# Ordering an expert layer's weights gate, up, then the down of the pair before, with outputs combined in five groups

## The chip, the cores and the metric

The kernel runs on one core of a Trainium2 chip. The metric is the time of one execution on the device, in microseconds (us).

## What is computed

The reference is a stack of four layers over 512 tokens of width 1024, in float32. Two of them end in a mixture of 16 experts, and only these two stages matter here. Every expert takes the 64 tokens with the highest affinity for it; what it returns is weighted with the gate and added back to the tokens:

```
x_e  = the 64 tokens that expert e chose                 (64 x 1024)
y_e  = (silu(x_e @ w_exp_gate[e]) * (x_e @ w_exp_up[e])) @ w_exp_down[e]
x    = x + gt_f * sum over e of  gate_e * y_e, put back to the tokens of e
```

Each of the three matrices of an expert is 1024 x 1024 in float32, 4 MB, so that one expert layer reads 192 MB of weights and uses each number for 64 tokens.

## The kernel before, in words

The engines run programs of their own, joined by semaphores. `Due` (line 182) counts for each engine how often it has already waited for a name, so that `due("y_sb")` is "the next y_sb".

**Weights.** All weights of the program are a list of panels, written in the order of their use; `expert_panels` (line 448) writes the part of an expert layer: 192 panels of 1,024 KB. The ring in SBUF has 8 slots. SP (line 513) issues one transfer per panel, in the order of the list, and before panel n it waits until TensorE has freed panel n - 8. TensorE takes panels in the same order with `panel()` (line 546). A product frees its panels through `free[0]`: the number is given to the next matmul that carries no signal of its own (line 531). Transposes (`turn`, line 541) never do this, and a matmul with a signal does not either.

**The expert stage.** The 16 experts go in 8 pairs p. A pair's two sets of 64 tokens stand side by side as 128 columns. On TensorE (`experts`, line 1063) the loop over pairs (line 1144) goes:

- `pair(0, x_sel, ...)`: the gate product into banks 0 and 1 of PSUM. A product takes 8 panels in four sub-steps of two panels.
- pairs 0 and 1: `turn_gates` (line 1096), which turns two tiles each of the gate weights through banks 6 and 7.
- pairs 3, 4, 6 and 7: `combine_blocks` (line 1134) for the outputs of three earlier pairs and half of the 8 feature blocks, through banks 6 and 7 in turn. VectorE adds each finished block to x (`add`, line 2156), and TensorE goes back to a bank after that.
- `pair(2, x_sel, ...)`: the up product into banks 2 and 3.
- `gather(p + 1)` (line 1105): the tokens of the next pair, 32 matmuls of 128 columns, into banks 6 and 7.
- the wait for `e_act`, the 8 transposes of the activations into banks 0 and 1, the wait for their copy (`aT_sb`), and `pair(4, e_actT, ...)`: the down product into banks 4 and 5.

After the loop the last two pairs are combined for all 8 blocks (line 1165).

ScalarE (line 1636) takes for each pair three steps on the gate (Exp, Ln, Exp; lines 1638 to 1640), the copies of the turned gates (1643), of the gathered tokens (1633), of the turned activations (1648), and of the down product into `y_store` (1650), which has room for 8 pairs. VectorE (line 2396) multiplies the gate in (2402), adds combined blocks to x (2405) and multiplies with up (2407).

Of the kernel before, what the change touches and what calls it, by code (L numbers as in the profile page):

```python
# [12 lines left out]
ACT = mybir.ActivationFunctionType  # L13
# [5 lines left out]
P = 128  # L19
D = 1024  # L20
KB = D // P
T = 512
# [261 lines left out]
def build(nc, args, out, par):  # L284
    a = args
    general, first_t, even_t, pool_t = (packed(t)[1] for t in constants())
    with ExitStack() as ctx:
# [30 lines left out]
        def cut(buffer, start, size, **shape):  # L318

            v = buffer[:, start:start + size]  # L320
            if not shape:
                return v
            names_ = " ".join(shape)
            return v.rearrange(f"p ({names_}) -> p {names_}", **shape)
# [77 lines left out]
        r_affT, r_thr_rows = two(work, 6144), work[:, 7168:7296]  # L402
        h_tok, sel = cut(mixflat, 0, 4096, n=4, f=D), cut(work, 0, 4096, n=4, c=D)
        r_pg, x_sel, e_act = work[:, 6144:7168], cut(work, 4096, 1024, k=KB, c=P), work[:, 5120:6144]
        r_pgT, y_store = cut(hbuf, 0, 4096, i=8, t=T), cut(proj_all, 0, 8192, i=8, d=D)
        e_actT, e_tmp = cut(proj_all, 8192, 1024, k=KB, c=P), proj_all[:, 9216:10240]


# [38 lines left out]

        def expert_panels(l):

            for e in range(0, E, 2):  # L450
                for w in ("w_exp_gate", "w_exp_up", "w_exp_down"):
                    for j in range(4):
                        for s in range(2):
                            v = a[w][l, e + s, 2 * j * P:(2 * j + 2) * P, :]
                            panels.append((v.rearrange("(k p) n -> p k n", p=P), 2, D))

        by_columns(a["w_in_even"][0], 2832)
        modulation_panels(PLANS["even"])
# [29 lines left out]
        def rounded(v):  # L488
# [1 line left out]
            return bass.AP(tensor=halves_of[v.tensor.name], offset=v.offset, ap=v.ap)  # L490


        combining = {3: (range(0, 3), range(0, 4)), 4: (range(0, 3), range(4, 8)),
                     6: (range(3, 6), range(0, 4)), 7: (range(3, 6), range(4, 8))}
        gate_tiles = {0: (0, 1), 1: (2, 3)}
        last_pairs = range(6, 8)

        def make_link(eng, name):

# [22 lines left out]
        def _(pe):  # L522
# [3 lines left out]
            def mm(o, lhsT, rhs, start, stop, signal=None, **kw):  # L526

                i = pe.matmul(o, lhsT, rhs, start=start, stop=stop, **kw)  # L528
                if signal:
                    i.then_inc(sem[signal], 1)  # L530
                elif free[0]:
                    i.then_inc(sem["panel_used"], free[0])
                    free[0] = 0
# [7 lines left out]
            def turn(o, i, signal=None, n=P):  # L541
                t = pe.transpose(o, i, ident[0:n, 0:n])  # L542
                if signal:
                    t.then_inc(sem[signal], 1)
# [518 lines left out]
            def experts(l):  # L1063
# [32 lines left out]
                def turn_gates(tiles):  # L1096

                    for n in tiles:
                        pe.wait_ge(*due("r_pg"))
                        for p in range(8):  # L1100
                            turn(ps[:, 6 + p // 4, p % 4 * P:p % 4 * P + P], r_pg[:, p * P:p * P + P],
                                 "r_pgT" if p == 7 else None)
                        pe.wait_ge(*due("r_pgT_sb"))
# [9 lines left out]
                def pair(banks, lhs, signal):  # L1113

                    for j in range(4):
                        w = [panel(), panel()]
                        for kk in range(2):
                            k = 2 * j + kk
                            for half in range(2):
                                for e in range(2):  # L1120
                                    s = slice(e * 64, e * 64 + 64)
                                    mm(ps[s, banks + half, :], lhs[:, k, s], w[e][:, kk, half * 512:half * 512 + 512],
                                       k == 0, k == KB - 1, signal if k == KB - 1 and half and e else None)
                        free[0] += 2

                unread = [0]

                def combine(pairs, m, bank):

                    for p in pairs:  # L1130
                        mm(ps[:, bank, :], y_store[:, p, m * P:m * P + P], r_pgT[:, p, :], p == pairs[0], p == pairs[-1],
                           "down" if p == pairs[-1] else None)

                def combine_blocks(pairs, blocks):
                    for m in blocks:
                        if unread[0] == 2:
                            pe.wait_ge(*due("down_x"))
                            unread[0] -= 1
                        combine(pairs, m, 6 + m % 2)
                        unread[0] += 1  # L1140

                pe.wait_ge(*due("r_marks"))
                gather(0)
                for p in range(8):
                    pe.wait_ge(*due("x_sel_sb"))
                    pair(0, x_sel, "e_gate")
                    turn_gates(gate_tiles.get(p, ()))
                    if p:
                        pe.wait_ge(*due("y_sb"))
                    if p in combining:  # L1150
                        combine_blocks(*combining[p])
                    pair(2, x_sel, "e_up")
                    if p < 7:
                        if unread[0]:
                            pe.wait_ge(*due("down_x", unread[0]))
                            unread[0] = 0
                        gather(p + 1)
                    pe.wait_ge(*due("e_act"))
                    for k in range(KB):
                        turn(ps[:, k // 4, k % 4 * P:k % 4 * P + P], e_act[:, k * P:k * P + P], "aT" if k == KB - 1 else None)  # L1160
                    pe.wait_ge(*due("aT_sb"))
                    pair(4, e_actT, "e_down")
                pe.wait_ge(*due("y_sb"))
                pe.wait_ge(*due("down_x", unread[0]))
                for m in range(KB):
                    combine(last_pairs, m, m)
                due("down_x", KB)

            def pooling():
# [81 lines left out]
        def _(act):  # L1251
# [367 lines left out]
            def experts():  # L1619
                act.wait_ge(*due("r_sub"))  # L1620
                to("r_exp", f(r_aff, r_aff, ACT.Exp))
                for i in range(8):
                    n, half = i // 2, i % 2
                    act.wait_ge(*due("r_tok"))
                    to("r_tok_sb", f(h_tok[:, n, half * 512:half * 512 + 512], ps[:, 4 + half, :], ACT.Copy))
                act.wait_ge(*due("r_affT"))
                to("r_affT_sb", f(r_affT[0:E, 0, :], ps[0:E, 1, :], ACT.Copy))
                act.wait_ge(*due("r_thr_rows"))
                to("r_thr_sb", f(r_thr, ps[:, 2, 0:E], ACT.Copy))

                def selected():
                    act.wait_ge(*due("x_sel"))
                    to("x_sel_sb", f(x_sel, ps[:, 6:8, :].rearrange("p b (i c) -> p (b i) c", i=4), ACT.Copy))  # L1633

                selected()
                for p in range(8):
                    act.wait_ge(*due("e_gate"))
                    link(f(e_tmp, ps[:, 0:2, :].rearrange("p b f -> p (b f)"), ACT.Exp, scale=-1.0))
                    link(f(e_tmp, e_tmp, ACT.Ln, bias=1.0))
                    to("e_exp", f(e_tmp, e_tmp, ACT.Exp, scale=-1.0))  # L1640
                    for n in gate_tiles.get(p, ()):
                        act.wait_ge(*due("r_pgT"))
                        to("r_pgT_sb", f(r_pgT[:, :, n * P:n * P + P],
                                         ps[:, 6:8, :].rearrange("p b (i t) -> p (b i) t", i=4), ACT.Copy))
                    if p < 7:
                        selected()
                    act.wait_ge(*due("aT"))
                    to("aT_sb", f(e_actT, ps[:, 0:2, :].rearrange("p b (i c) -> p (b i) c", i=4), ACT.Copy))  # L1648
                    act.wait_ge(*due("e_down"))
                    to("y_sb", f(y_store[:, p, :], ps[:, 4:6, :].rearrange("p b f -> p (b f)"), ACT.Copy))  # L1650

            def layer(l):
                if l:
# [82 lines left out]
        def _(dve):  # L1736
# [607 lines left out]
            def experts(gate):  # L2344
# [51 lines left out]
                for p in range(8):  # L2396
                    for n in gate_tiles.get(p, ()):
                        dve.wait_ge(*due("r_pgT"))
                        if n < NT - 1:
                            gated(n + 1)  # L2400
                    dve.wait_ge(*due("e_exp"))
                    link(tt(e_tmp, e_tmp, ps[:, 0:2, :].rearrange("p b f -> p (b f)"), ALU.mult))  # L2402
                    if p in combining:
                        for m in combining[p][1]:
                            add(gate, m, 6 + m % 2, "down", "down_x")
                    dve.wait_ge(*due("e_up"))
                    to("e_act", tt(e_act, e_tmp, ps[:, 2:4, :].rearrange("p b f -> p (b f)"), ALU.mult))

            def pooling():

# [134 lines left out]
```

## Time and profile before

| what | value |
|---|---|
| time before, median of 3 runs | 3923.52 us (3921.61 to 3927.85) |
| the profiled execution's own time | 3919.22 us |
| its span, first to last instruction | 3917.4 us |
| TensorE matmuls busy | 3312.8 us (85%) |
| VectorE busy | 1424.9 us (36%) |
| ScalarE busy | 932.7 us (24%) |
| read from HBM | 632.48 MB, 162 GB/s over the span |
| mean granted clock of TensorE | 0.906 |

The shares are over the whole program, in which stages with different limits follow each other. The two expert stages are the last but one group of slices and the last group; they alone stream weights at nearly 400 GB/s, while the stages between them read little. "PE" is TensorE's matmuls, "PEld" its weight loads, "DVE" VectorE, "ACT" ScalarE, "SPq" the queue of SP. A float32 matmul stands in the trace as two records. Line 528 is the helper that issues every matmul, line 542 the one of every transpose, so products are told apart by what they read: `ring,work` is a gate or up product, `ring,proj` a down product, `work,mix` the gathering, `h,proj` the combining.

### The profile page before, as it was taken

How to read it: one execution, taken by the hardware profiler on the slowest of the kernel's cores; microseconds unless marked ns; L12 is line 12 of the kernel's file. 1: busy time of each engine (PE TensorE's matmuls, PEld its weight loads, DVE VectorE, ACT ScalarE, POOL GpSimd, SP SyncE). 2: the span in 40 equal slices, each digit the busy share in tenths (PEclk: the TensorE clock that was granted, in tenths of full speed). 3: DMA queues.
4: the chain of work that ended last, by engine and by line, in shares of the span. 5: the costliest groups of instructions: out<-in, count | busy, mean ns of one | idle time of the engine just before them, and what ended most of it. 6: DMA issues, size and time to landing. Idle time of an engine off the chain costs nothing. (4 is left out here: it accounts for less than half of the span.)

```text
span 3917.4 us, 38069 instructions
## 1 busy us (share of the span) xinstructions
PE 3312.8 (85%) x16560; PEld 2204.8 (56%) x16560; DVE 1424.9 (36%) x1841; ACT 932.7 (24%) x1395; POOL 0.2 (0%) x4
## 2 busy tenths in 40 slices
PE   6986879998996779999898967578898986789897
PEld 3765758886765766887454726454434344434342
DVE  3446437653546636762002365730000024200001
ACT  3542132233633223221203511111010021010101
POOL 0000000000000000000000000000000000000000
PEclk9996989999996989999998967679999997899999
DMA  6370012322261012323111090018999950499996
GB/s 228 96 269 1 1 42 88 97 86 79 86 238 63 1 33 76 97 92 109 44 54 33 3 401 27 4 39 321 395 389 391 382 213 32 192 396 390 395 384 238
DMA packets 247383, 637.05 MB, mean 163 GB/s; under 512 B 12849, under 2 KB 110129, under 8 KB 247089
## 3 DMA queue, kind: packets, MB, share of 16 engines
q1 hardware_dynamic: 244128, 627.22, 43.0%
q10 hardware_dynamic: 3088, 7.40, 0.5%
q8 instruction: 131, 2.15, 0.2%
q14 instruction: 36, 0.29, 0.0%
HBM read 632.48 MB, written 2.10 MB: 162 GB/s over the span
## 5 line engine op out<-in xcount | busy, mean ns | idle before, releaser
L528 PE MATMUL ps<-ring,work 128*64 128x512 f32 (+1 forms) x3584 | 585.7, 542 | 137.8 <-DMA ring<-in_w_exp_gate 51.2
L528 PE MATMUL ps<-mix_halves,work_halves 128*128 128x512 f32 (+1 forms) x1456 | 585.4, 402 | 29.6 <-DVE h_halves L1790 29.5
L528 PE MATMUL ps<-h_halves,work_halves 128*128 128x512 f32 (+1 forms) x1456 | 573.3, 394 | 34.5 <-DVE mix_halves L1790 34.5
L528 PE MATMUL ps<-mix_halves,ring_halves 128*128 128x512 f32 x1264 | 495.1, 392 | 0.0
L528 PEld LDWEIGHTS ps<-ring,work 128*64 128x64 f32 (+1 forms) x3584 | 207.0, 133 | 501.1 <-issue 401.7
L1790 DVE TENSOR_TENSOR ring_halves<-ring,work_halves 128x2048 fp32r<-128x2048 f32 x108 | 239.1, 2214 | 302.4 <-ACT work_halves L1273 301.6
L528 PEld LDWEIGHTS ps<-mix_halves,work_halves 128*128 128x128 f32 (+1 forms) x1456 | 274.9, 189 | 110.3 <-issue 30.8
L528 PEld LDWEIGHTS ps<-h_halves,work_halves 128*128 128x128 f32 (+1 forms) x1456 | 275.9, 189 | 99.6 <-issue 42.6
L1273 ACT ACTIVATE work_halves<-ring 128x2048 fp32r<-128x2048 f32 x108 | 199.6, 1849 | 487.3 <-PE ps L528 390.9
L528 PEld LDWEIGHTS ps<-mix_halves,ring_halves 128*128 128x128 f32 x1264 | 237.9, 188 | 52.3
L528 PE MATMUL ps<-ring,proj 128*64 128x512 f32 x1024 | 226.4, 600 | 18.5 <-ACT proj L1648 16.2
L2402 DVE TENSOR_TENSOR proj<-proj,ps 128x1024 f32<-128x1024 f32 x16 | 19.5, 1220 | 530.2 <-ACT proj L1640 522.5
L1752 DVE RECIPROCAL work<-work 128x512 f32<-128x512 f32 (+1 forms) x56 | 181.4, 3239 | 1.9
L528 PE MATMUL ps<-work,proj 128*128 128x128 f32 (+1 forms) x912 | 148.8, 321 | 38.2 <-DVE work L2122 13.8
L528 PE MATMUL ps<-h,proj 128*128 128x512 f32 (+2 forms) x384 | 166.7, 576 | 4.6 <-issue 2.3
L528 PE MATMUL ps<-h,ring 128*128 128x512 f32 (+1 forms) x368 | 161.8, 598 | 5.6 <-ACTq L1264 5.6
L528 PEld LDWEIGHTS ps<-ring,proj 128*64 128x64 f32 x1024 | 73.8, 138 | 160.8 <-issue 141.3
L528 PEld LDWEIGHTS ps<-work,proj 128*128 128x128 f32 (+1 forms) x912 | 129.2, 213 | 57.2 <-issue 15.6
L528 PE MATMUL ps<-work,consts 128*128 128x512 f32 (+1 forms) x188 | 110.5, 738 | 49.8 <-ACT work L1307 34.4
L542 PE MATMUL ps<-consts,work 128*128 128x128 f32 x530 | 87.8, 310 | 70.4 <-DVE work L2364 24.4
L528 PE MATMUL ps<-proj_halves,work_halves 128*128 128x512 f32 x352 | 136.9, 389 | 0.0
L528 PEld LDWEIGHTS ps<-work,mix 128*128 128x128 f32 x1024 | 119.8, 198 | 22.1 <-issue 11.4
(354 smaller groups left out, 3602.9 us busy)
## 6 DMA issues: line engine op xcount, KB each, us to landing
ring<-in_w_exp_gate SPq DMA_DIRECT2D x128, 1024.0 KB, 8.8
ring<-in_w_exp_up SPq DMA_DIRECT2D x128, 1024.0 KB, 13.0
ring<-in_w_exp_down SPq DMA_DIRECT2D x128, 1024.0 KB, 10.5
ring<-in_ada_w SPq DMA_DIRECT2D x48, 1024.0 KB, 9.2
ring<-in_w_mod SPq DMA_DIRECT2D x48, 1024.0 KB, 16.8
ring<-in_w_in SPq DMA_DIRECT2D x22, 1024.0 KB, 5.3
ring<-in_w_gate SPq DMA_DIRECT2D x22, 1024.0 KB, 5.3
ring<-in_w_up SPq DMA_DIRECT2D x22, 1024.0 KB, 5.4
```

The lines of the kernel that those rows point to most:

```text
L528: i = pe.matmul(o, lhsT, rhs, start=start, stop=stop, **kw)
L542: t = pe.transpose(o, i, ident[0:n, 0:n])
L1273: to("hi", f(rounded(panel_high(splits[0])), slot(n), ACT.Copy))
L1752: link(dve.reciprocal(v, v))
L1790: to("lo", tt(rounded(v), v, rounded(hi), ALU.subtract))
L2402: link(tt(e_tmp, e_tmp, ps[:, 0:2, :].rearrange("p b f -> p (b f)"), ALU.mult))
```

## The change

Pairs are pipelined by one product: the down product of pair p - 1 comes after the up product of pair p, and the panels are listed in that order. The activations of pair p - 1 are turned between gate p and up p, into banks 6 and 7. Turning the gate tiles moves behind the up product. `y_store` keeps four pairs. Combining comes in five groups: pairs 0 and 1 before up 3, pairs 2 and 3 before up 5, pairs 4 and 5 before up 7, each over all 8 blocks; pair 6 before down 7, in four banks; pair 7 at the end. Each group but the last now ends with a wait until VectorE has added its last blocks.

```diff
-        r_pgT, y_store = cut(hbuf, 0, 4096, i=8, t=T), cut(proj_all, 0, 8192, i=8, d=D)
+        r_pgT, y_store = cut(hbuf, 0, 4096, i=8, t=T), cut(proj_all, 0, 4096, i=4, d=D)
...
         def expert_panels(l):
-            for e in range(0, E, 2):
-                for w in ("w_exp_gate", "w_exp_up", "w_exp_down"):
-                    for j in range(4):
-                        for s in range(2):
-                            v = a[w][l, e + s, 2 * j * P:(2 * j + 2) * P, :]
-                            panels.append((v.rearrange("(k p) n -> p k n", p=P), 2, D))
+            def product(w, p):
+                for j in range(4):
+                    for s in range(2):
+                        v = a[w][l, 2 * p + s, 2 * j * P:(2 * j + 2) * P, :]
+                        panels.append((v.rearrange("(k p) n -> p k n", p=P), 2, D))
+
+            for p in range(8):
+                product("w_exp_gate", p)
+                product("w_exp_up", p)
+                if p:
+                    product("w_exp_down", p - 1)
+            product("w_exp_down", 7)
...
-        combining = {3: (range(0, 3), range(0, 4)), 4: (range(0, 3), range(4, 8)),
-                     6: (range(3, 6), range(0, 4)), 7: (range(3, 6), range(4, 8))}
+        combining = {3: (0, 1), 5: (2, 3), 7: (4, 5)}
         gate_tiles = {0: (0, 1), 1: (2, 3)}
-        last_pairs = range(6, 8)
...
-                unread = [0]
-
                 def combine(pairs, m, bank):
                     for p in pairs:
-                        mm(ps[:, bank, :], y_store[:, p, m * P:m * P + P], r_pgT[:, p, :], p == pairs[0], p == pairs[-1],
+                        mm(ps[:, bank, :], y_store[:, p % 4, m * P:m * P + P], r_pgT[:, p, :], p == pairs[0], p == pairs[-1],
                            "down" if p == pairs[-1] else None)
-                def combine_blocks(pairs, blocks):
-                    for m in blocks:
-                        if unread[0] == 2:
+                def combine_blocks(pairs, banks):
+                    for m in range(KB):
+                        if m >= banks[1]:
                             pe.wait_ge(*due("down_x"))
-                            unread[0] -= 1
-                        combine(pairs, m, 6 + m % 2)
-                        unread[0] += 1
+                        combine(pairs, m, banks[0] + m % banks[1])
+                    pe.wait_ge(*due("down_x", banks[1]))
+
+                def turn_act():
+                    for k in range(KB):
+                        turn(ps[:, 6 + k // 4, k % 4 * P:k % 4 * P + P], e_act[:, k * P:k * P + P], "aT" if k == KB - 1 else None)
...
                 for p in range(8):
                     pe.wait_ge(*due("x_sel_sb"))
+                    if p:
+                        pe.wait_ge(*due("e_act"))
                     pair(0, x_sel, "e_gate")
-                    turn_gates(gate_tiles.get(p, ()))
-                    if p:
+                    if p >= 2:
                         pe.wait_ge(*due("y_sb"))
                     if p in combining:
-                        combine_blocks(*combining[p])
+                        combine_blocks(combining[p], (6, 2))
+                    if p:
+                        turn_act()
                     pair(2, x_sel, "e_up")
+                    if p:
+                        pe.wait_ge(*due("aT_sb"))
+                    turn_gates(gate_tiles.get(p, ()))
                     if p < 7:
-                        if unread[0]:
-                            pe.wait_ge(*due("down_x", unread[0]))
-                            unread[0] = 0
                         gather(p + 1)
-                    pe.wait_ge(*due("e_act"))
-                    for k in range(KB):
-                        turn(ps[:, k // 4, k % 4 * P:k % 4 * P + P], e_act[:, k * P:k * P + P], "aT" if k == KB - 1 else None)
-                    pe.wait_ge(*due("aT_sb"))
-                    pair(4, e_actT, "e_down")
+                    if p:
+                        pair(4, e_actT, "e_down")
+                pe.wait_ge(*due("e_act"))
+                turn_act()
                 pe.wait_ge(*due("y_sb"))
-                pe.wait_ge(*due("down_x", unread[0]))
+                combine_blocks((6,), (0, 4))
+                pe.wait_ge(*due("aT_sb"))
+                pair(4, e_actT, "e_down")
+                pe.wait_ge(*due("y_sb"))
                 for m in range(KB):
-                    combine(last_pairs, m, m)
+                    combine((7,), m, m)
                 due("down_x", KB)
```

On ScalarE the copy of the turned activations now stands right behind the three steps on the gate, and the copy of the down product of pair p - 1 behind that of the gathered tokens (for p = 7, and once more at the end). On VectorE the adds of a group cover all 8 blocks and stand, as before, behind the multiplication at line 2402; 8 adds of pair 6 follow the loop.

## Rows read from the trace of the kernel before

**Rows 1.** The page: the span, and the issues of the gate panels.

```profile
span 3917.4 us, 38069 instructions
...
ring<-in_w_exp_gate SPq DMA_DIRECT2D x128, 1024.0 KB, 8.8
```

**Rows 2.** Windows of the first expert stage; last columns: granted clock, DMA share, GB/s.

```profile
2660.60:3121.50 460.90, 406.46 (x1989) 178.03 (x1985) 29.68 (x29) 46.58 (x46) 0.00 (x0) 0.98 0.98 388
2660.60:2859.20 198.60, 170.24 (x860) 75.69 (x856) 10.91 (x9) 22.18 (x22) 0.00 (x0) 0.96 0.99 392
2886.00:2896.00 10.00, 8.85 (x70) 6.89 (x70) 0.00 (x0) 1.94 (x2) 0.00 (x0) 1.00 1.03 410
...
2873.50:2877.00 3.50, 3.50 (x20) 1.22 (x18) 0.00 (x0) 0.00 (x0) 0.00 (x0) 1.00 0.54 142
2939.50:2942.00 2.50, 2.50 (x14) 0.85 (x12) 0.00 (x0) 0.00 (x0) 0.00 (x0) 1.00 0.87 247
3067.50:3072.00 4.50, 4.50 (x24) 1.51 (x22) 0.00 (x0) 0.00 (x0) 0.00 (x0) 1.00 0.27 66
...
2897.00:2900.50 3.50, 3.50 (x18) 1.15 (x16) 0.00 (x0) 0.00 (x0) 0.00 (x0) 1.00 0.39 104
...
3092.00:3096.00 4.00, 4.00 (x22) 1.40 (x20) 0.00 (x0) 0.00 (x0) 0.00 (x0) 1.00 0.41 100
```

**Rows 3.** TensorE in order of time, gate 3 to down 3: start us, us.

```profile
2855.66 3.65 PE L528 MATMUL ps<-ring,work 128*64 128x512 f32 x16 [1.47 <-DMA ring<-in_w_exp_gate]
2859.25 10.82 PE L528 MATMUL ps<-h,proj 128*128 128x512 f32 x24
2870.00 13.95 PE L528 MATMUL ps<-ring,work 128*64 128x512 f32 x64
2883.88 7.41 PE L528 MATMUL ps<-work,mix 128*128 128x128 f32 x64
2891.13 1.04 PE L542 MATMUL ps<-consts,work 128*128 128x128 f32 x8
2893.32 13.95 PE L528 MATMUL ps<-ring,proj 128*64 128x512 f32 x64 [1.16 <-ACT proj L1648]
```

**Rows 4.** TensorE's waits, first expert stage: total us, times, longest us.

```profile
PE ps L528 <- DMA ring<-in_w_exp_gate: 26.1, 18, 2.8
```

**Rows 5.** TensorE in order of time, from the end of gate 7.

```profile
3121.48 10.82 PE L528 MATMUL ps<-h,proj 128*128 128x512 f32 x24
...
3147.51 1.09 PE L542 MATMUL ps<-consts,work 128*128 128x128 f32 x8 [1.32 <-DVE work L2407]
...
3166.40 13.97 PE L528 MATMUL ps<-h,proj 128*128 128x512 f32 x32 [1.16 <-issue]
```

**Rows 6.** ScalarE and VectorE in order of time, after gate 3.

```profile
2859.36 1.03 ACT L1638 ACTIVATE proj<-ps 128x1024 f32<-128x1024 f32 x1 [17.52 <-PE ps L528]
...
2861.50 1.06 ACT L1640 ACTIVATE proj<-proj 128x1024 f32<-128x1024 f32 x1
...
2862.59 1.22 DVE L2402 TENSOR_TENSOR proj<-proj,ps 128x1024 f32<-128x1024 f32 x1 [43.81 <-ACT proj L1640]
2863.84 1.61 DVE L2158 SCALAR_TENSOR_TENSOR x<-ps,small,x 128x512 f32<-128x512 f32 x2
```

**Rows 7.** TensorE around the gate tiles of pair 0; SP's first refill; landing times.

```profile
2668.10 1.09 PE L542 MATMUL ps<-consts,work 128*128 128x128 f32 x8
...
2675.51 15.38 PE L528 MATMUL ps<-ring,work 128*64 128x512 f32 x64 [1.16 <-issue]
...
2658.75 0.88 SPq L516 DMA_DIRECT2D ring<-in_w_exp_up  x2
...
DMA to landing us min/median/max: 4.8/8.8/13.7
```

**Rows 8.** TensorE behind its longest wait for panels, and the window of those sub-steps.

```profile
2793.32 8.78 PE L528 MATMUL ps<-ring,work 128*64 128x512 f32 x32 [2.77 <-DMA ring<-in_w_exp_gate]
...
2794.50:2797.90 3.40, 3.40 (x10) 1.21 (x8) 0.00 (x0) 0.00 (x0) 0.00 (x0) 0.50 1.03 411
```

More of the change, by code:

```diff
@@ L1633, in selected, with turned, stored @@
                     to("x_sel_sb", f(x_sel, ps[:, 6:8, :].rearrange("p b (i c) -> p (b i) c", i=4), ACT.Copy))
+                def turned():
+                    act.wait_ge(*due("aT"))
+                    to("aT_sb", f(e_actT, ps[:, 6:8, :].rearrange("p b (i c) -> p (b i) c", i=4), ACT.Copy))
+                def stored(p):
+                    act.wait_ge(*due("e_down"))
+                    to("y_sb", f(y_store[:, p % 4, :], ps[:, 4:6, :].rearrange("p b f -> p (b f)"), ACT.Copy))
                 selected()
@@ L1640, in experts @@
                     to("e_exp", f(e_tmp, e_tmp, ACT.Exp, scale=-1.0))
+                    if p:
+                        turned()
                     for n in gate_tiles.get(p, ()):
@@ L1646, in experts @@
                         selected()
[L1647 to L1650, printed above, removed]
+                    if p:
+                        stored(p - 1)
+                turned()
+                stored(7)
             def layer(l):
@@ L2403, in experts @@
                     if p in combining:
-                        for m in combining[p][1]:
+                        for m in range(KB):
                             add(gate, m, 6 + m % 2, "down", "down_x")
@@ L2407, in experts @@
                     to("e_act", tt(e_act, e_tmp, ps[:, 2:4, :].rearrange("p b f -> p (b f)"), ALU.mult))
+                for m in range(KB):
+                    add(gate, m, m % 4, "down", "down_x")
             def pooling():
```

## The prediction

> **What bounds the kernel now.** I read the page's head first [rows 1]: the profiled execution spans 3917.4 us, and its own time was 3919.2 us, 4.3 us under the median of the three runs (3923.5 us). The sum below is a difference, made on the profiled execution and then put on the median. Only the two expert stages change; the first runs from 2654 to 3180 us, the second has the same instructions, and the sum is made once and doubled.
>
> Next come the windows of the queue [rows 2]. While it is fed, the queue moves 410 GB/s, so a panel of 1,024 KB (1.049 MB) takes 2.56 us. From the first refill (2660.6 us) to the last panel of gate 7 that TensorE has to wait for (about 3121.5 us) the mean is 388 GB/s: the queue stands still for 460.9 x (1 - 388/410) = 24.7 us of 460.9. A pair of experts takes 24 panels, 24 x 2.56 = 61.4 us of queue, and costs TensorE less than that: the weights bound this stage. TensorE's list shows the same from its side: before a gate product's sub-steps it waits for panels some 1.47 us each [rows 3], 26.1 us in 18 waits before gate panels [rows 4].
>
> So the stage's length is: panels x 2.56, plus the queue's standstills, plus what TensorE does after the last panel it waited for. The ring holds 8 panels, 20.5 us of queue. A standstill comes where TensorE frees nothing for so long that all 8 slots fill. I call any stretch between two products a pause.
>
> **What a pause costs.** After gate 3 the pause is the combining, 2859.25 to 2870.00 = 10.75 us [rows 3]. The queue's dips after three such pauses are 3.5 x (1 - 142/410) = 2.3, 2.5 x (1 - 247/410) = 1.0 and 4.5 x (1 - 66/410) = 3.8 us [rows 2], mean 2.4; the fourth is like the first. By then the ring is full, so each further microsecond of pause is a microsecond of standstill: after a product that was itself waiting for panels, **idle = pause - 8.4**. A second kind of dip follows the pause for gather and turn, 2883.88 to 2893.32 = 9.4 us, entered with panels in hand: 2.6, 2.6 and 3.0 us (first and last of three in [rows 2]), so idle = pause - 6.7. The rest is at the start: 198.6 x (1 - 392/410) = 8.7 us until gate 3 ends.
>
> **The change, part by part (one expert stage).**
>
> *The long pause between gate and up in pairs 3, 5 and 7.* It now holds 8 blocks of two matmuls, in two banks, and the turning of the activations. A matmul of 512 columns costs 13.97/16 = 0.87, back to back 0.86 us [rows 5] (the profile lists each as two records). Blocks 0 and 1 take 3.4 us. Block 2 needs VectorE's add of block 0, and this stands behind the chain Exp, Ln, Exp on ScalarE and a multiply on VectorE: the chain starts at 2859.36, the add at 2863.84 and the pair of adds takes 1.61 us [rows 6], so TensorE can go on at 5.6 us after the gate's end: 2.2 us of waiting (with three matmuls a block this wait was only some 0.5 us). Blocks 2 to 7: 6 x 1.72 = 10.3. The new wait for both last adds: 0.9 (0.75 of add and its signals). Behind it on TensorE is the turning, 1.04 [rows 3], and behind this the up product; nobody else waits. Sum 3.4 + 2.2 + 10.3 + 0.9 + 1.04 = 17.9 us against 10.75. Idle 17.9 - 8.4 = 9.5 us, three times: **28.5 us**.
>
> *The pause between up and down, pairs 1 to 6.* The turning and the wait for its copy (1.15 us, end of turn to 2893.32) leave it; gather alone is 2883.88 to 2891.13 = 7.3 us. Behind an up product that was short of panels that is under 8.4: no dip. Behind the full ring after pairs 3 and 5 it is 7.3 - 6.7 = 0.6 us, twice: **1.2 us**. Moved activations, their copy and the x_sel copy lie under whole products of 13.95 us; were that cover gone, each would cost about 1.2 us.
>
> *The start.* Turning two gate tiles moves from behind gate 0 (and 1) to behind up 0 (and 1). It took 2668.10 to 2675.51 = 7.4 us [rows 7], of which some 2.5 us was waiting for ScalarE's chain; this is long done behind the up product. Two turns of 1.04, a copy or gate multiply between (1.3) and the copy after (1.15) give 4.6; I take 5.0, with 7.4 as the other end. Pauses then: 5.0 + 7.3 + 1.15 (the x_sel copy, uncovered here) = 13.4 before gate 1, and 12.3 before down 0. Idle 5.0 + 3.9 = **8.9 us**, against 8.7 now: the same.
>
> *The queue in all:* 28.5 + 1.2 + 8.9 = 38.6 us against 24.7: **+13.9 us**. SP issues the same 192 transfers, in another order; its wait for a slot stays the only one in that queue.
>
> *The tail.* Now the last panel that TensorE waits for belongs to gate 7; from this product's end to the last combining it is 3121.48 to 3166.40 + 13.97 = 58.9 us [rows 5]. After the change the last such panel is down 6's, 8 panels later (**+20.5 us**), and then come: the y_sb copy with the turning beside it 1.16, 8 matmuls 6.9, the last add 0.9, down 7 13.95, the copy 1.16, 8 matmuls 6.9 = 30.9 us, **-28.0 us**. In that pause nothing frees the last two slots, since its matmuls all carry a signal of their own and transposes free nothing: down 7's last two panels are issued only at its first matmul. From issue to landing a transfer takes 4.8 us at least [rows 7], plus 2.56 for the second and about 1 until the issue: 8.4 us, needed after 10.5 us. Covered, by 2 us.
>
> *Sum.* +13.9 + 20.5 - 28.0 = **+6.4 us a stage, +13 us in all**: 3919.2 + 13 = 3932 for the profiled execution, 3923.5 + 13 = **3936.5 us** on the median, 0.33% slower. A measurement of this kernel can tell about 0.2% (7.8 us) from no change.
>
> **Unknowns and their ends.** The 2.2 us wait inside the combining may cost the clock too: behind a wait of 2.77 us the sub-steps took 8.78 us for 32 records, not 7.0, at a granted clock of 0.50, the lower level, 1.2 GHz [rows 8]. That is 1.7 us in each long pause, at most +10 in all; other waits of 1.5 us are followed by full clock, so I take nothing. The gate tiles at 7.4 instead of 5.0: +4.8 a stage, +10 in all. The other way, the smallest dip seen (1.0) instead of 2.4: -4.2 a stage, -8 in all.
>
> **The rivals.**
> 1. *Forecast: the ring runs full in three long pauses.* For it: each shorter pause of the same place already shows a dip. 0.55, with 3925 to 3946 as its own range.
> 2. *The same, and the half clock in the pauses or the long gate tiles.* +13 + 10 to 20 = +23 to +33: 3946 to 3956. For it: the row at 0.50 clock; against: the many waits near 1.5 us keep the full clock. 0.13.
> 3. *The dips don't grow one for one* (the smallest dips, cheap gate tiles): +6.4 - 4.2 = +2 a stage, 3928, no change. 0.18.
> 4. *Other side: TensorE's own path is what counts.* Per stage it loses 7 waits for the copy (8.1), the wait for the last activations (1.3 [rows 5]) and 4.8 at the gate tiles; it gains 1.15 at x_sel and, in combining, 3 x 16.9 + 8.9 - 1.2 + 6.9 = 65.3 against 4 x 10.8 + 14.0 = 57.2, +8.1. Net -5.0, -10 in all: 3913.5. It decides if panel waits (26.1 us for gate panels) do not grow with the longer pauses, which needs a queue with spare time: 24.7 us of standstill says that there is a little, 61.4 us a pair that there is not much. 0.14.
>
> On the rate, the trace shows 410 GB/s [rows 2]. The Trainium skill (DMA: Bandwidth & Descriptors, Where 436 GB/s comes from) puts the ceiling at 435 GB/s. By that rule a panel would be 2.40 us, an estimate: the ring would be full 1.3 us sooner, at seven dry places after against twelve now (-6.5 us), and the 8 panels of the tail 1.3 us cheaper, so the sum would be about -1 us a stage, no change. No window here holds that rate; it would be one more way to rival 3.
>
> That the change does not do what it says is not to be feared: the order of panels and products is in the code.
>
> **How the numbers follow.** Slower by over 0.2% is rivals 1 and 2 less the edge of 1: 0.65. Within 0.2%: rival 3 and that edge, 0.22. Faster: 0.13. The range, 3911 to 3956, takes in the ends above and rival 4's value.
>
> **What the changed profile would show.** In each stage: three pauses of about 18 us from a gate's end to the first matmul of the up product, with block 2 waiting about 2 us for VectorE; a dip of 8 to 10 us in the queue behind each; the dips behind gather nearly gone; mean rate from first refill to down 6's last panel about 377 GB/s (176 x 1.049 MB in 176 x 2.56 + 38.6 us); 31 us from down 6 to the end of combining. The prediction is wrong if these dips are short, if up 0 does not wait for panels, or if down 7 waits for its last pair.

## The result, and the profile after

The changed kernel takes 3935.7 us (median of 9 runs, 3929.9 to 3943.8) against 3923.5 us before (9 runs, 3915.5 to 3927.9): ratio 1.0033, 95% interval 1.0022 to 1.0044. It is slower, by a third of a percent. The profiled execution took 3929.9 us, with a span of 3928.1 us.

The two expert stages, from the first matmul of gate 0 to the last combining, took 526.2 and 523.3 us before and take 530.9 and 529.4 us now, 10.8 us more in all. The rest of the program is the same, 2867.9 and 2867.7 us. So the whole difference of the two spans, 10.7 us, lies in the two stages.

TensorE in order of time after the change, gate 3 to down 2, and then the end of the stage (start us, us, instruction, in brackets the idle time before it and what ended it); it answers to [rows 3] and [rows 5]:

```profile
2836.39 3.65 PE L532 MATMUL ps<-ring,work 128*64 128x512 f32 x16 [1.47 <-DMA ring<-in_w_exp_gate]
2839.97 3.70 PE L532 MATMUL ps<-h,proj 128*128 128x512 f32 x8
2845.37 10.57 PE L532 MATMUL ps<-h,proj 128*128 128x512 f32 x24 [1.70 <-DVE x L2178]
2856.78 1.10 PE L546 MATMUL ps<-consts,work 128*128 128x128 f32 x8 [0.84 <-DVE x L2178]
2857.81 13.95 PE L532 MATMUL ps<-ring,work 128*64 128x512 f32 x64
2871.69 7.41 PE L532 MATMUL ps<-work,mix 128*128 128x128 f32 x64
2879.04 13.95 PE L532 MATMUL ps<-ring,proj 128*64 128x512 f32 x64
...
3154.88 1.09 PE L546 MATMUL ps<-consts,work 128*128 128x128 f32 x8
3156.07 7.13 PE L532 MATMUL ps<-h,proj 128*128 128x512 f32 x16
3164.09 13.95 PE L532 MATMUL ps<-ring,proj 128*64 128x512 f32 x64 [0.89 <-issue]
3179.16 7.13 PE L532 MATMUL ps<-h,proj 128*128 128x512 f32 x16 [1.11 <-ACT proj L1651]
```

The second row is blocks 0 and 1 of the combining, the third blocks 2 to 7, after a wait for VectorE's add. From the gate's end to the up product it is 2857.81 - 2839.97 = 17.8 us, against 10.75 before. At the end, down 7 runs through its 64 records without a wait for panels.

The windows of the same stage after the change (columns as in [rows 2]): first refill to the end of down 6; first refill to the end of gate 3; the two dips of the start; then, in order of time, the three long dips and the two dips behind gather.

```profile
2661.60:3154.90 493.30, 429.23 (x2077) 186.98 (x2073) 40.89 (x43) 49.25 (x48) 0.00 (x0) 0.99 0.95 378
2661.60:2840.00 178.40, 153.11 (x789) 69.51 (x785) 10.91 (x9) 20.46 (x20) 0.00 (x0) 0.98 0.98 389
2700.00:2709.00 9.00, 9.00 (x44) 3.02 (x46) 0.00 (x0) 0.00 (x0) 0.00 (x0) 1.00 0.67 251
2745.00:2754.00 9.00, 9.00 (x50) 3.74 (x50) 0.00 (x0) 1.03 (x1) 0.00 (x0) 1.00 0.47 167
2853.00:2866.00 13.00, 12.15 (x53) 4.58 (x53) 1.80 (x3) 1.02 (x1) 0.00 (x0) 1.00 0.33 121
2883.00:2887.00 4.00, 4.00 (x22) 1.39 (x20) 0.00 (x0) 0.00 (x0) 0.00 (x0) 1.00 0.88 317
2986.00:2999.00 13.00, 12.15 (x55) 4.67 (x55) 1.70 (x3) 1.02 (x1) 0.00 (x0) 1.00 0.36 123
3015.00:3020.00 5.00, 5.00 (x26) 1.72 (x24) 0.00 (x0) 0.00 (x0) 0.00 (x0) 1.00 0.94 342
3119.00:3132.00 13.00, 12.15 (x55) 4.73 (x55) 1.61 (x3) 1.02 (x1) 0.00 (x0) 1.00 0.34 121
```

At 410 GB/s as the full rate, each long dip is 13 x (1 - 121/410) = 9.2 us of standstill, where the kernel before had 1.0 to 3.8 us. The dips behind gather are down to 4 x (1 - 317/410) = 0.9 and 5 x (1 - 342/410) = 0.8 us. In all the queue stands still for 493.3 x (1 - 378/410) = 38.5 us, against 24.7. The granted clock in the windows of the long dips is 1.00.

### The profile page after: what moved, and what is told of

Read it like the earlier page. It is cut to its first block and busy times, and to the rows that moved or that the text cites. A ratio compares the mean times of both kernels' runs of the same rounds, so it can differ in the third digit from the quotient of the medians.

```text
span 3928.1 us, 38102 instructions
## 1 busy us (share of the span) xinstructions
PE 3307.7 (84%) x16560; PEld 2205.9 (56%) x16560; DVE 1449.0 (37%) x1873; ACT 933.7 (24%) x1395; POOL 0.2 (0%) x4
## 5 line engine op out<-in xcount | busy, mean ns | idle before, releaser
L532 PE MATMUL ps<-work,proj 128*128 128x128 f32 (+1 forms) x912 | 149.2, 322 | 38.3 <-DVE work L2142 13.9
L532 PE MATMUL ps<-h,proj 128*128 128x512 f32 (+2 forms) x384 | 166.3, 576 | 14.9 <-DVE x L2178 10.2
L2178 DVE SCALAR_TENSOR_TENSOR x<-ps,small,x 128x512 f32<-128x512 f32 x128 | 93.4, 749 | 178.1 <-PE ps L532 174.5
L532 PE MATMUL ps<-work,consts 128*128 128x512 f32 (+1 forms) x188 | 108.6, 728 | 49.8 <-ACT work L1317 34.4
L532 PE MATMUL ps<-work,mix 128*128 128x128 f32 x1024 | 124.3, 285 | 15.4 <-DVE work L2406 10.6
## 6 DMA issues: line engine op xcount, KB each, us to landing
ring<-in_w_exp_up SPq DMA_DIRECT2D x128, 1024.0 KB, 12.3
```

Of the source, the lines that this page charges most:

```text
L2178: to(done, stt(out=x[:, m, :], in0=ps[:, bank, :], scalar=gate[:, m:m + 1], in1=x[:, m, :], op0=ALU.mult, op1=ALU.add))
```

## The experiments

All are compared by their medians, with the kernel before run on the same chip beside them (its medians there were 3920.9 to 3922.7 us); the ratios are against that. Where a few microseconds matter, the lengths of the two expert stages in the profiles are given as well, since what lies outside them moved between 2867 and 2879 us from one profile to the next, without any edit there. The changed kernel was not run beside them. The kernel before was 0.8 to 2.7 us faster there than the 3923.5 us above, so a difference between a run's median and the changed kernel's 3935.7 us is uncertain by about as much.

**1. Half groups.** The same outputs are combined in two halves of four blocks.

```diff
-        combining = {3: (0, 1), 5: (2, 3), 7: (4, 5)}
+        combining = {3: ((0, 1), range(0, 4)), 4: ((0, 1), range(4, 8)), 5: ((2, 3), range(0, 4)),
+                     6: ((2, 3), range(4, 8)), 7: ((4, 5), range(0, 4))}
...
+                    if p == 7:
+                        combine_some((4, 5), range(4, 8), late_banks)
```

> The changed kernel, but each group of two pairs is combined in two halves of four blocks (pairs 3 to 7, and once behind up 7), still in two banks. Ring theory (idle of the queue = pause - 8.4 us behind a gate product): the pause becomes 3.4 + 2.2 + 3.4 + 0.9 + 1.04 = 11.0 us, so 2.6 us of standstill five times and 0.6 us behind gather four times, 24.5 us a stage instead of 38.6: 28 us less in all than the changed kernel, about 3908 us. Rival, TensorE's own path sets the time: five waits for VectorE of 3.1 us instead of three, so 12 us more than the changed kernel, about 3948 us.

Measured: 3911.1 us, ratio 0.9970 (0.9958 to 0.9981). More waits for VectorE, and still 25 us less than the changed kernel. The rival, which wanted 3948, is out. Four of the five dips in that profile:

```profile
2922.00:2929.00 7.00, 7.00 (x34) 2.29 (x32) 0.00 (x0) 0.00 (x0) 0.00 (x0) 1.00 0.81 297
2986.00:2994.00 8.00, 8.00 (x40) 2.59 (x38) 0.00 (x0) 0.52 (x1) 0.00 (x0) 1.00 0.79 291
3052.00:3058.00 6.00, 6.00 (x30) 2.00 (x28) 0.00 (x0) 0.00 (x0) 0.00 (x0) 1.00 0.73 267
3116.00:3122.00 6.00, 6.00 (x30) 2.00 (x28) 0.00 (x0) 0.00 (x0) 0.00 (x0) 1.00 0.81 293
```

They are 1.9, 2.3, 2.1 and 1.7 us, where 2.6 were expected; the first, behind gate 3, is 16 x (1 - 347/410) = 2.5 us.

**2. Six banks.** The long groups stay whole, but the blocks go to banks 4, 5, 2, 3, 6, 7.

```diff
+        some_banks = (4, 5, 2, 3, 6, 7)
...
-                        combine_blocks(combining[p], (6, 2))
+                        combine_some(combining[p], range(KB), some_banks)
+                        read(4)
```

> The changed kernel with its three long groups whole, but over six banks (4, 5, 2, 3, 6, 7), so that no matmul waits for an add inside the pause. Ring theory: the pause falls from 17.8 to 6.9 + 6.9 + 1.04 = 14.8 us, the standstill from 9.1 to 6.2 us, 18 us less in all: about 3917 us. If the clock or the wait itself were the cost and not the length of the pause, the queue's dip would keep its 9 us.

Measured: 3916.4 us, ratio 0.9985 (0.9974 to 0.9996). TensorE's list and the windows of the three dips:

```profile
2844.17 14.00 PE L533 MATMUL ps<-h,proj 128*128 128x512 f32 x32
2858.01 1.04 PE L547 MATMUL ps<-consts,work 128*128 128x128 f32 x8
```

```profile
2857.00:2867.00 10.00, 10.00 (x49) 3.91 (x49) 1.00 (x2) 1.02 (x1) 0.00 (x0) 1.00 0.40 146
2987.00:2997.00 10.00, 10.00 (x49) 3.91 (x49) 0.84 (x2) 1.02 (x1) 0.00 (x0) 1.00 0.45 163
3117.00:3127.00 10.00, 10.00 (x50) 3.87 (x51) 0.75 (x1) 1.02 (x1) 0.00 (x0) 1.00 0.44 160
```

The wait is gone from the combining, the pause is 2858.98 - 2844.17 = 14.8 us, and the dips are 6.4, 6.0 and 6.1 us. It is the length of the pause that counts.

**3. Both.** Half groups over banks 2, 3, 4, 5 (and 0, 1, 6, 7 behind up 7). As in run 2, the waits for the adds that are still open stand behind the up product.

> As the kernel in halves, but the four blocks go into four banks that are free at that time, so TensorE waits for no add inside the pause. Ring theory: pause 6.9 + 1.04 = 7.9 us, below 8.4, no standstill behind gate products or gather; only the 9 us at the start stay. 29.5 us a stage less than the changed kernel, 59 in all: about 3877 us (3870 to 3890). Rival, TensorE's own path: only the waits go, 3 x 3.0 us a stage, 18 us in all: about 3918 us.

Measured: 3881.5 us, ratio 0.9901 (0.9886 to 0.9916), with all the work done. One pause and the window around it, and the window from the first of these pauses to down 6:

```profile
2837.21 7.13 PE L534 MATMUL ps<-h,proj 128*128 128x512 f32 x16
2844.18 1.04 PE L548 MATMUL ps<-consts,work 128*128 128x128 f32 x8
2845.15 13.95 PE L534 MATMUL ps<-ring,work 128*64 128x512 f32 x64
```

```profile
2840.00:2853.00 13.00, 13.00 (x57) 5.24 (x57) 4.04 (x5) 1.54 (x2) 0.00 (x0) 1.00 1.03 410
...
2837.00:3127.00 290.00, 273.06 (x1291) 116.31 (x1290) 29.30 (x34) 29.01 (x28) 0.00 (x0) 1.00 1.02 408
```

The pause is 7.9 us, and the queue runs through it at 410 GB/s. For 290 us it loses next to nothing (408 of 410).

**4. No combining of pairs 0 to 5.** `combining = {}`.

> The changed kernel without the combining of pairs 0 to 5 (their outputs are not added to x; pairs 6 and 7 are). Takes 16.8 us of TensorE out of three pauses of a stage, 50 us a stage. Ring theory: only the queue's standstill can be won, 3 x 9.1 + 2 x 0.6 = 28.5 us a stage, 57 in all: about 3879 us, and the waits for panels grow. Rival, TensorE's own path: 101 us less, about 3835 us.

Measured: 3878.2 us, ratio 0.9892 (0.9877 to 0.9906). 50 us of TensorE's work and waiting taken out of each stage, 101 in all, gave 57 us, about what the queue had stood still in the pauses (3 x 9.2 + 0.9 + 0.8 = 29.3 us a stage). The waits for the panels of up products grew from 22.1 us (in the changed kernel) to

```profile
PE ps L532 <- DMA ring<-in_w_exp_up: 34.9, 27, 2.9
```

Run 3 does all the combining and is only 3 us slower than this.

**5. Four more matmuls, in the long pauses or in the short ones.** `mm(ps[:, 6, :], y_store[:, 0, 0:P], r_pgT[:, 0, :], True, True)` four times, at the end of the combining, or between gate and up of pairs 2, 4 and 6.

> The changed kernel with four further matmuls (3.4 us, into a bank that is written anew) at the end of the combining in pairs 3, 5 and 7. Ring theory: those pauses already fill the ring, each grows from 17.8 to 21.3 us, and all of it is standstill: 3.4 x 6 = 21 us more than the changed kernel, about 3956 us. TensorE's own path says the same here; it is the pair to dup_short.

> The changed kernel with the same four matmuls between gate and up of pairs 2, 4 and 6, where the pause is only 1.04 us. Ring theory: 4.5 us is below 8.4, the ring does not fill, TensorE only waits less for panels: no change, about 3936 us. Rival, TensorE's own path: 21 us more, about 3956 us.

Measured: 3956.4 us (ratio 1.0090, 1.0074 to 1.0105) in the long pauses, 3937.1 us (1.0035, 1.0022 to 1.0048) in the short ones. The same 24 matmuls cost 21 us in one place and 1.4 us, within the spread of the runs, in another (23.6 and 3.5 us by the lengths of the stages). First the dips of the former, then three windows of the latter over the lengthened short pauses:

```profile
2856.00:2872.00 16.00, 15.15 (x64) 5.74 (x65) 0.75 (x1) 1.02 (x1) 0.00 (x0) 1.00 0.27 96
2992.00:3008.00 16.00, 15.15 (x64) 5.82 (x64) 1.12 (x2) 1.03 (x1) 0.00 (x0) 1.00 0.26 91
```

```profile
2780.00:2792.00 12.00, 12.00 (x52) 4.85 (x50) 1.22 (x1) 4.16 (x4) 0.00 (x0) 1.00 1.03 410
2914.00:2926.00 12.00, 12.00 (x53) 4.84 (x51) 1.22 (x1) 4.16 (x4) 0.00 (x0) 1.00 1.03 410
3046.00:3058.00 12.00, 12.00 (x52) 4.87 (x50) 1.22 (x1) 4.16 (x4) 0.00 (x0) 1.00 1.02 409
```

**6. The old order without that combining.** The kernel before with `combining = {}`.

> The kernel before, old order, without the combining of pairs 0 to 5 (not added to x; pairs 6 and 7 are at the end). It stands to the run no_mid (3878 us) as the order alone. Ring theory: the pause of gather, turning and copy is 9.4 us behind an up product that waits for panels, 1.0 us of standstill in six pairs, 8.7 at the start, so 10 us less than in the kernel before; and the tail falls by 4.4 us (up 7 now waits for panels): 14.4 us a stage, 29 in all, about 3893 us, 15 us above no_mid. Rival, the order is worth nothing: as no_mid, 3878 us. If TensorE's path set the time, 44 us of combining a stage would be won, about 3835 us.

Measured: 3899.4 us, ratio 0.9940 (0.9923 to 0.9956), 21 us above run 4. The two stages took 512.3 and 510.3 us, 26.9 us less than in the kernel before (28.8 expected); the rest of the difference from 3893 us is outside them (2875.5 us in this profile). So the new arrangement is worth some 20 us where nothing of pairs 0 to 5 is combined (by the stages: 512.3 + 510.3 against 501.9 + 502.2, 18.5 us), and the changed kernel gives it back. The expectation's "order alone" says too much: run 4 also turns the gate tiles behind the up product, and it combines pair 6 before down 7, where the old kernel combines pairs 6 and 7 at the end. The ends of the first stage, from the last of its first 184 panels on, first in this run and then in run 4:

```profile
3136.09 3.65 PE L527 MATMUL ps<-ring,work 128*64 128x512 f32 x16 [1.46 <-DMA ring<-in_w_exp_up]
...
3161.46 13.97 PE L527 MATMUL ps<-h,proj 128*128 128x512 f32 x32 [1.16 <-issue]
```

```profile
3124.50 3.65 PE L532 MATMUL ps<-ring,proj 128*64 128x512 f32 x16 [1.44 <-DMA ring<-in_w_exp_down]
...
3152.36 7.13 PE L532 MATMUL ps<-h,proj 128*128 128x512 f32 x16 [1.11 <-ACT proj L1651]
```

That tail is 35.7 us here and 31.3 us in run 4 (35.9 and 31.3 in the second stage): 8.9 us of the 18.5. The other 9.7 lie before it, 476.7 us from the stage's start against 470.6, and 474.4 against 470.8; the queue stands still there for 474.9 x (1 - 398/410) = 13.9 us in the first stage here and 464.5 x (1 - 403/410) = 7.9 us in run 4.

**7. Pair 6 combined at the end.**

```diff
-                combine_blocks((6,), (0, 4))
...
-                    combine((7,), m, m)
+                    combine((6, 7), m, m)
```

> The changed kernel with pair 6 combined together with pair 7 at the end, instead of before down 7. By the ledger of the queue: the pause before down 7 shrinks from 9.2 to 2.2 us, but down 7 then waits for its panels (its last pair lands 20.5 us after down 6's), so it ends 20.5 us after down 6, and 1.2 + 13.9 us of combining follow: 35.6 us from down 6 to the last combining instead of 31.4. 4.2 us more a stage, 8 in all, about 3944 us. Rival, TensorE's own path: the same matmuls in another place, one wait of 0.9 us less, about 3934 us.

Measured: 3950.4 us, ratio 1.0064 (1.0042 to 1.0086). The sign and the mechanism are those of the ledger (the sum over the queue and the tail), the size is not: 14.7 us more than the changed kernel by the medians, 13.3 by the stages, not 8. The end of the second stage in that profile:

```profile
3890.55 1.09 PE L546 MATMUL ps<-consts,work 128*128 128x128 f32 x8
3892.94 3.65 PE L532 MATMUL ps<-ring,proj 128*64 128x512 f32 x16 [1.30 <-DMA ring<-in_w_exp_down]
3897.20 3.65 PE L532 MATMUL ps<-ring,proj 128*64 128x512 f32 x16 [0.61 <-DMA ring<-in_w_exp_down]
3902.32 3.65 PE L532 MATMUL ps<-ring,proj 128*64 128x512 f32 x16 [1.47 <-DMA ring<-in_w_exp_down]
3908.17 5.35 PE L532 MATMUL ps<-ring,proj 128*64 128x512 f32 x16 [2.20 <-DMA ring<-in_w_exp_down]
3914.73 13.97 PE L532 MATMUL ps<-h,proj 128*128 128x512 f32 x32 [1.21 <-ACT proj L1650]
```

Down 7 now waits for its panels, as expected. In the second stage its last sub-step waits 2.2 us and then takes 5.35 instead of 3.65 us, at a granted clock of 0.72 in the window from 3908 to 3914 us, and this tail is 38.2 us, not 35.6. In the first stage no sub-step is slow, and it is 36.9 us: down 7 starts 6.3 us after the sub-step before it, where the panels of two sub-steps take 5.12 us of queue. Against 31.4 us in each stage of the changed kernel the tails give 12 of the 13 us, the two stages taken together (by stage they gave 5.5 and 6.8 us, and the stages grew by 3.5 and 9.7).

**8. The second gate tile through banks 4 and 5,** on top of run 3.

```diff
-                            turn(ps[:, 6 + p // 4, p % 4 * P:p % 4 * P + P], r_pg[:, p * P:p * P + P],
+                            turn(ps[:, 6 - 2 * (n % 2) + p // 4, p % 4 * P:p % 4 * P + P], r_pg[:, p * P:p * P + P],
...
-                        pe.wait_ge(*due("r_pgT_sb"))
+                        if n % 2 == 0:
+                            pe.wait_ge(*due("r_pgT_sb"))
```

> The kernel of halves_banks (3881 us), with the second gate tile of a pair turned into banks 4 and 5, so that its copy is waited for only before the down product. The pauses at the start fall from 13.3 and 12.1 us by about 1.2 us each. Ring theory: 1.2 us less standstill twice a stage, 5 us in all, about 3877 us; it is the only standstill left. If the start is not what bounds the rest, no change: 3881 us.

Measured: 3877.9 us, ratio 0.9887 (0.9873 to 0.9902). It is 3.6 us below run 3, but the ranges of the two (3879.2 to 3884.9 and 3874.3 to 3881.3) overlap. The two pauses of the first stage did shrink as expected, from 13.3 and 12.1 to 11.9 and 10.6 us. The stages are less clear: the first took 504.2 us against 503.6 in run 3, the second 500.9 against 506.7, and 3.0 of those 5.8 us are a gathering that took 10.29 us in run 3 and 7.31 here. So the shorter pauses are shown, and their gain in time is not. It is the fastest version found, 1.1% faster than the kernel before and 58 us faster than the changed one, with all the work done.

## Why the prediction was right

The forecast was 3936.5 us, and 3935.7 us was measured. The number alone would prove little, since a sum of gains and losses can agree by chance; the parts and the runs say whether it did.

- **The bound.** The queue of weights bounds the stage. Run 5 shows it (the same work free in one place, at full price in another), and run 4 (101 us of TensorE's path removed, 57 gained).
- **The long pause.** 17.9 us worked out, 17.8 measured: the first wait is 1.70 us (2.2 in the sum), the wait at the end 0.84 (0.9), and blocks 2 to 7 are 10.57 us in the profile (10.3).
- **Idle = pause - 8.4.** The rule said 9.5 us a dip, and 9.2 came. The kernels give it five points and a bound, all behind a gate product that waited for panels:

| kernel | pause, us | mean standstill, us | pause less standstill |
|---|---|---|---|
| half groups, four banks | 7.9 | 0 | at least 7.9 |
| before | 10.75 | 2.4 | 8.4 |
| half groups | 11.0 | 2.1 | 8.9 |
| six banks | 14.8 | 6.2 | 8.6 |
| changed | 17.8 | 9.2 | 8.6 |
| four more matmuls | 21.3 | 12.3 | 9.0 |

  From 11 to 21 us of pause the standstill grows by 10.2 us: one for one. The constant is nearer to 8.8 than to the 8.4 that three uneven dips gave.
- **The pause for gather.** 0.6 us twice was forecast, 0.9 and 0.8 were measured.
- **The start.** 8.9 us forecast, 178.4 x (1 - 389/410) = 9.1 measured, but this agreement is partly luck. The pause before gate 1 is 13.3 us (13.4), and its dip is 3.5 us (9 x (1 - 251/410)), where pause - 8.4 gave 5.0: the rule doesn't hold there, and why was not tested. The pause before down 0 is 13.7, not 12.3, and its dip 5.3 (9 x (1 - 167/410)), not 3.9: gather took 9.01 us there instead of 7.4, with a granted clock of 0.76 in the window from 2737 to 2744 us. The two misses cancel.
- **The queue in all.** 38.6 us forecast, 38.5 measured in the first stage, 491.7 x (1 - 380/410) = 36.0 in the second.
- **The tail.** 30.9 us forecast, 3179.16 + 7.13 - 3154.88 = 31.4 measured. Down 7's last two panels were in time, as worked out. Run 7 shows that the place of pair 6's combining matters as the ledger says.
- **The sum.** +6.4 us a stage; +4.8 and +6.1 measured, +10.8 in all instead of +13. Most of what is missing is in the first stage. From the first refill to the last panel waited for, it took 493.3 us against 460.9, 32.4 more, where 13.9 + 20.5 = 34.4 were forecast; the tail fell by 27.5, not 28.0. Whether the standstill or the 8 panels were the smaller can't be told: the rates are rounded to 1 GB/s, which is 1.2 us over 490 us.

Of the rivals, the half clock inside the pause did not come: after the 1.70 us wait, 24 records took 10.57 us, 0.44 us each, as without a wait. Nor did the long gate tiles: the two turns with their waits took 2691.40 - 2686.63 = 4.8 us, near the 5.0 of the sum. The length of one wait does not settle the clock. In run 7 the sub-step behind a wait of 2.2 us was slow (5.35 us); in the changed kernel's first stage the one behind a wait of 3.00 us, at 2728.88 us, took the usual 3.65 us. The dips that do not grow one for one are refuted by the table. TensorE's own path as the bound is refuted by runs 1, 4 and 5. The Trainium skill's ceiling of 435 GB/s (DMA: Bandwidth & Descriptors, Where 436 GB/s comes from) would, as a rate and by the estimate in the prediction, have meant no change. This stream does not reach it: over 290 us almost without a standstill (run 3) the queue moved 408 GB/s.

Of the signs named in advance, the dips, the mean rate (378 GB/s, 377 forecast) and down 7 came as said, and up 0 does wait for panels (1.46 us twice).

What the prediction did not say is what the rearrangement is worth without the grouping. Runs 4 and 6 show some 20 us: about half because the queue stands still less, about half in a shorter tail. That the first half comes from the copy of the activations and its wait leaving the pauses fits the rows, but was not varied by itself. The loss is in the grouping, whose three long pauses a stage cost 2 x 3 x 9.2 = 55 us of standstill.

## What to carry to other kernels

When a ring of buffers feeds a stage and the queue is its bound, count each stretch in which the consumer frees nothing, not its total work: here a pause shorter than the ring's slack (8.4 to 9.0 us behind a product that waited for panels) cost nothing, and each microsecond beyond it cost a microsecond. Splitting one pause of 17.8 us into two of 11.0 us gained 25 us (run 1), free PSUM banks that took the waits out of the whole pause gained 19 us (run 2), and both together, two pauses of 7.9 us, gained 54 us (run 3). The slack is read from the dips that the queue already has.

## What was not expected

- **Late panels.** In most sub-steps that wait for panels the wait is 1.47 us, but now and then one is 2.6 to 3.0 us, with the queue at its full rate (409 GB/s from 2782 to 2794 us, around the one below). One before the change is in [rows 8], one after stands in TensorE's list in order of time:

```profile
2785.16 8.78 PE L532 MATMUL ps<-ring,work 128*64 128x512 f32 x32 [2.62 <-DMA ring<-in_w_exp_up]
```

  Its 32 records take 8.78 us, as those in [rows 8], at a granted clock of 0.86 in that window. Neither kernel has many such waits, and what delays these panels was not tested.
- **The spread.** What lies outside the expert stages varied by 12 us between profiles of kernels that are the same there. Comparing the lengths of the stages separated 18.5 from 21 us in run 6.
